# Final norm from one square per block, the forget gates' chain moved behind K's norms, and a weight tile between sums and spread at the FFN norm

## The reference

```
h = [meta; x]                                   # 528 x 1024
hn = rms_norm(h, attn_norm)
q, k, v, gate, f = split(hn @ fox_w_in)         # 16 heads of 64
q, k = rms_norm per head
c = cumsum(log_sigmoid(f + b_f))                # per head, along the tokens
s = q.k / 8 + c_q - c_k, causal                 # softmax, times v, times sigmoid(gate)
h = h + o @ fox_w_out
h = h + swiglu(rms_norm(h, ffn_norm))           # hidden width 2816
h = rms_norm(h, final_norm)[16:]                # x of the second block
n1 = rms_norm(h, norm1_g) * (1 + sc1) + sh1     # sc, sh from silu(c) @ w_ada
h = h + g1 * mixer(n1)                          # conv branch of 31 taps, state space branch
h = h + g2 * moe(rms_norm(h, norm2_g) * (1 + sc2) + sh2)   # 64 experts, top 2
out = rms_norm(h, final_g)
```

## Time and profile before

| | |
|---|---|
| median of 3 runs | 2474.2 us (2468.7 to 2475.04) |
| the profiled execution | 2477.98 us, of which the span from the first to the last instruction is 2476.2 |
| PE busy | 2295.3 us (93%), mean granted clock 0.969 |
| DVE, ACT, POOL busy | 1030.7, 723.5, 780.0 us |
| chain that ended last | PE 55%, DMA 29%, DVE 11%, ACT 3% |
| DMA | 599.45 MB, some 425 GB/s from about 1550 us on |

### The profile page before, as it was taken

One profiled execution on the slowest core, in us unless ns is written; L12 is line 12 of the kernel. 1 busy time (PEld: TensorE's weight loads), 2 busy tenths in 40 slices (PEclk: granted clock), 3 DMA queues, 4 the chain that ended last, 5 costly groups with the idle time before them and its releaser, 6 DMA issues.

```text
span 2476.2 us, 26324 instructions
## 1 busy us (share of the span) xinstructions
PE 2295.3 (93%) x10666; PEld 1436.1 (58%) x10666; DVE 1030.7 (42%) x1701; ACT 723.5 (29%) x1165; POOL 780.0 (32%) x493
## 2 busy tenths in 40 slices
PE   8999999999999999999999998988888888888885
PEld 5677678888887787777777783323233232323222
DVE  2736545543445999846675323111111111111113
ACT  4435643222224333557774231100000000100001
POOL 4235645564553343433326611111111000000100
PEclk9999999999999999999999998999999999999997
DMA  5131233644644443243444268999999999999996
GB/s 178 44 133 65 83 116 102 204 145 157 204 124 103 102 102 98 82 145 128 136 150 192 93 246 341 423 424 424 424 424 425 427 426 425 426 426 426 427 426 258
DMA packets 174776, 599.45 MB, mean 242 GB/s; under 512 B 17733, under 2 KB 96581, under 8 KB 148928
## 3 DMA queue, kind: packets, MB, share of 16 engines
q1 hardware_dynamic: 155568, 564.39, 58.7%
q10 hardware_dynamic: 8416, 23.92, 2.5%
q0 software_dynamic: 10672, 9.46, 1.2%
HBM read 593.19 MB, written 28.97 MB: 251 GB/s over the span
## 4 chain that ended last, share of the span: by engine, by line
PE 55%; DMA 29%; DVE 11%; ACT 3%; issue 1%; POOL 1%; SPq 0%; ACTq 0%; DVEq 0%; POOLq 0%
DMA arena<-in_w 21%; PE ps L828 11%; PE ps L830 11%; PE ps L829 11%; PE ps L1361 7%; DMA ring<-in_w 6%; DVE ps L2311 5%; PE ps L1359 2%; PE ps L1380 1%; PE ps L1063 1%; PE ps L879 1%; PE ps L1041 1%; PE ps L1032 1%; PE ps L929 1%; PE ps L1007 1%
## 5 line engine op out<-in xcount | busy, mean ns | idle before, releaser
L2759 POOL TENSOR_TENSOR ring_r<-ring,ring_r 128x1024 fp32r<-128x1024 f32 (+2 forms) x215 | 510.3, 2381 | 674.2 <-ACT ring_r L1455 674.0
L828 PE MATMUL ps<-r,ring_r 128*128 128x512 f32 (+2 forms) x1496 | 598.3, 400 | 1.5 <-DVE arena L2299 1.2
L830 PE MATMUL ps<-r,ring_r 128*128 128x512 f32 (+2 forms) x1496 | 585.2, 391 | 0.0
L829 PE MATMUL ps<-r,ring_r 128*128 128x512 f32 (+2 forms) x1496 | 584.9, 391 | 0.0
L1466 ACT ACTIVATE arena<-ps 128x512 f32<-128x512 f32 (+5 forms) x239 | 159.1, 688 | 1073.9 <-PE ps L1361 851.1
L1361 PE MATMUL ps<-arena 128*64 128x512 f32 x672 | 317.2, 628 | 69.5 <-DMA arena<-in_w 69.2
L1359 PE MATMUL ps<-arena 128*64 128x512 f32 x672 | 329.6, 640 | 0.0
L1455 ACT ACTIVATE ring_r<-ring 128x1024 fp32r<-128x1024 f32 x220 | 222.5, 1014 | 354.3 <-PE ps L830 201.1
L828 PEld LDWEIGHTS ps<-r,ring_r 128*128 128x128 f32 (+2 forms) x1496 | 280.8, 188 | 72.5 <-issue 11.7
L2874 POOL DMA_INDIRECT y_d<-arena,cbm x64 | 63.9, 999 | 815.7 <-DVE arena L2713 557.1
L829 PEld LDWEIGHTS ps<-r,ring_r 128*128 128x128 f32 (+2 forms) x1496 | 280.8, 188 | 63.5 <-issue 5.0
(11 more groups left out here) (377 smaller groups left out, 2612.7 us busy)
## 6 DMA issues: line engine op xcount, KB each, us to landing
arena<-in_w SPq DMA_DIRECT2D x106, 2048.0 KB, 35.9
ring<-in_w SPq DMA_DIRECT2D x86, 2048.0 KB, 37.0
ring<-in_w_ada SPq DMA_DIRECT2D x12, 2048.0 KB, 7.9
ring<-in_ffn_w_in SPq DMA_DIRECT2D x22, 1024.0 KB, 7.7
ring<-in_w_in SPq DMA_DIRECT2D x40, 512.0 KB, 6.1
ring<-in_w_in SPq DMA_DIRECT2D x8, 2048.0 KB, 9.2
ring<-in_fox_w_in SPq DMA_DIRECT2D x7, 2048.0 KB, 8.5
arena<-acs_d SPq DMA_DIRECT2D x16, 512.0 KB, 3.7
```

Source lines behind the costliest of these rows:

```text
L828: e.matmul(out, wh[:, k, :], X.hi[:, k0 + k, :], start=first and k == 0, stop=False)
L829: e.matmul(out, wh[:, k, :], X.lo[:, k0 + k, :], start=False, stop=False)
L830: m = e.matmul(out, wl[:, k, :], X.hi[:, k0 + k, :], start=False, stop=last and k == nk - 1)
L2759: e.tensor_tensor(GL[t], grans[t][1], GH[t].bitcast(F32), ALU.subtract).then_inc(sem["gr_lo"], 1)
```

## The change

Forget gates: `log1p_rest` is cut into pieces (`forget_part`) that DVE runs behind `head_norm("v", j)` for j = 4 to 7, of which only j = 4 still has a norm. `FL` moves to free space, `SEL2` is made by ACT near the start, and PE and ACT no longer wait for `cscan`. FFN norm: PE makes `hg1` between the sums and the spread, and `hu1` behind it. Final norm: ACT squares h once, one block earlier and ahead of its split, and makes `x2` itself; DVE keeps two sums of that one square, plain and weighted by final_norm² + eps (`G2E`), the last block being left to PE; PE sums the weighted row first, in two banks, then the spread, and the plain row around it; its root is taken behind n1; the fillers shrink from 10, 2 and 4 matmuls to 2 (each shows as two instructions in the trace). Four banks are taken in place of two.

```diff
@@ -232,10 +232,11 @@
     for half, (k0, nk) in enumerate(HALVES):
         for nt in range(k0, k0 + nk):
             t("hg", nt)
+            if nt == 1:
+                t("fnb")
             t("hu", nt)
             if nt == 0:
                 t("fn")
-                t("fnb")
             for n in ada_done(half, nt):
                 t("adb", n)
         for nt in range(8):
@@ -243,7 +244,9 @@
             for n in ada_out(half, nt):
                 t("adb", n)
     t("fin")
+    t("fin7")
     t("finb")
+    t("finq")
     for j in range(2):
         t("taps", j, bank=6 + j)
     taps = {6, 7}
...
-        FL = view(30656, 4, L)[0:16]
+        FL = view(23872, 4, L)[0:16]
...
+        FACC, G2E = HTM[0:2], P("attn_norm")
+
+        def square_of(name, k):
+
+            if name == "fin":
+                return FACC[0] if k == 0 else HTM[2 + k % 2]
+            return ACC if k == 0 else TMP[k % 2]
...
+            def columns_of(out, tts, *terms):
+
+                for tt in tts:
+                    for x, weight in terms:
+                        m = e.matmul(out[:, tt:tt + 1], x[:, 128 * tt:128 * tt + 128], weight, start=x is terms[0][0], stop=x is terms[-1][0])
+                return m
...
                 w.wait_ge(u.free, u.n)
-                w.wait_ge(sem["cscan"], 3)
+                w.wait_ge(sem["sc"], 3)
...
             sums_by_token("fn")
+            whole("hg", 1, X=XF)
             spread("fn", "fnb")
+            whole("hu", 1, X=XF)
             for half, (k0, nk) in enumerate(HALVES):
                 for nt in range(k0, k0 + nk):
-                    if nt > 0:
+                    if nt > 1:
                         whole("hg", nt, X=XF)
...
                             ada_columns(n)
-            fill(10, "fin")
-            sums_by_token("fin")
-            fill(2, "finb")
+            rows0, adds0, nk = sums["fin"]
+            u, u7, uq, x7 = ps("fin"), ps("fin7"), ps("finq"), square_of("fin", 7)
+            w.wait_ge(sem["sq_used"], adds0 + 2 * (nk - 2))
+            for use in (u, u7, uq):
+                w.wait_ge(use.free, use.n)
+            columns_of(u.ap, range(4), (FACC[1], ones[:, 0:1])).then_inc(u.full, 1)
+            w.wait_ge(sem["sq"], rows0 + nk)
+            columns_of(u7.ap, range(4), (x7, G2E[:, 7:8])).then_inc(u7.full, 1)
+            columns_of(uq.ap, range(2), (FACC[0], ones[:, 0:1]), (x7, ones[:, 0:1]))
             spread("fin", "finb")
-            fill(4, *conv_tiles(0)[0])
+            columns_of(uq.ap, range(2, 4), (FACC[0], ones[:, 0:1]), (x7, ones[:, 0:1])).then_inc(uq.full, 1)
+            fill(2, *conv_tiles(0)[0])

...
                 e.activation(hnH[:, k, :], TMP[k % 2][:, NM:L], ACT.Copy).then_inc(sem["hn_hi"], 1)
             w.wait_ge(sem["param"], 16)
             e.activation(SC, P("c"), ACT.Silu).then_inc(sem["sc"], 1)
+            for hh in range(2):
+                e.activation(SEL2[:, NM * hh:NM * hh + NM], C("sel16"), ACT.Copy).then_inc(sem["sc"], 1)
             w.wait_ge(sem["hn"], 8)
...
-            w.wait_ge(sem["cscan"], 1)
             next_tile()
             for nt in range(AHEAD):
...
             def squares_fin(k):
 
                 square_after(ps("fo", 1, k), "fin", k, hT[:, k, NM:L])
-                square_row("fin", k, hT[:, k, NM:L], T, 1, pc("final_norm", k))
+                if k == 7:
+                    e.activation(ST[:, 12:13], C("eps"), ACT.Sqrt)
+                e.activation(x2[:, k, :], hT[:, k, NM:L], ACT.Identity, scale=pc("final_norm", k)).then_inc(sem["x2"], 1)
...
                 for i in range(16):
+                    if half == 1 and i % 2 == 1 and i >= 3:
+                        squares_fin(i // 2 - 1)
                     next_tile()
-                    if half == 1 and i % 2 == 1 and i >= 5:
-                        squares_fin(i // 2 - 2)
-            for k in (6, 7):
-                squares_fin(k)
-            e.activation(ST[:, 12:13], C("eps"), ACT.Sqrt)
+            squares_fin(7)
             u = ps("fin")
             w.wait_ge(sem["dg"], diags["fin"] - 1)
-            w.wait_ge(u.full, u.n + 1)
-            e.activation(ST[:, 4:8], u.ap[:, 4:8], ACT.Sqrt, scale=1.0 / D, bias=C("eps2"))
-            evict(ST[:, 8:12], u, ACT.Sqrt, src=u.ap[:, 0:4], scale=1.0 / D, bias=C("eps"))
+            w.wait_ge(u.free, u.n + 1)
+            e.activation(ST[:, 4:8], ST[:, 4:8], ACT.Sqrt, scale=1.0 / D, bias=C("eps2")).then_inc(ps("fin7").free, 1)
             w.wait_ge(sem["x2"], 8)
             e.dma_start(a["x2_d"], x2).then_inc(sem["spill"], 16)
...
             for k in range(8):
                 w.wait_ge(sem["n1"], k + 1)
                 e.activation(n1H[:, k, :], TMP[k % 2][:, :T], ACT.Identity, bias=modcol(0, k)).then_inc(sem["n1_hi"], 1)
+            u = ps("finq")
+            evict(ST[:, 8:12], u, ACT.Sqrt, src=u.ap[:, 0:4], scale=1.0 / D, bias=C("eps"))
...
+                e.tensor_tensor(acc, acc, square_of(name, k)[:, :n], ALU.add).then_inc(sem["sq_used"], 1)
+
+            def add_final(k):
+
+                rows0, adds0, nk = sums["fin"]
+                x, gain = square_of("fin", k), G2E[:, k:k + 1]
+                w.wait_ge(sem["sq"], rows0 + k + 1)
+                if k == 0:
+                    e.tensor_scalar(FACC[1], x, gain, None, ALU.mult).then_inc(d.next(), 1)
+                    last()
+                    return
+                if k >= 2:
+                    w.wait_ge(sem["sq_used"], adds0 + 2 * (k - 1))
+                e.scalar_tensor_tensor(FACC[1], x, gain, FACC[1], ALU.mult, ALU.add).then_inc(sem["sq_used"], 1)
+                e.tensor_tensor(FACC[0], FACC[0], x, ALU.add).then_inc(sem["sq_used"], 1)
 
             def low(name, k, dst, src, hi, hi_sem, value):
...
                 w.wait_ge(u.free, u.n + 1)
             log1p_exp(FL[:, 0, :], FL[:, 1, :])
-            log1p_rest(FL[:, 1, :], FL[:, 2, :], FL[:, 3, :], 1)
-            e.scalar_tensor_tensor(FL[:, 1, :], FL[:, 0, :], 0.0, FL[:, 3, :], ALU.min, ALU.subtract).then_inc(d.next(), 1)
-            last()
-            e.tensor_tensor_scan(cT, C("ones", 0, 16)[:, 0:1].broadcast_to([16, L]), FL[:, 1, :], 0.0, ALU.mult, ALU.subtract).then_inc(sem["cscan"], 1)
-            w.wait_ge(sem["cscan"], 1)
-            for hh in range(2):
-                e.tensor_copy(SEL2[:, NM * hh:NM * hh + NM], C("sel16")).then_inc(sem["cscan"], 1)
+
+            def forget_part(j):
+
+                if j == 4:
+                    log1p_ratio(FL[:, 1, :], FL[:, 2, :], FL[:, 3, :], 1)
+                if j == 5:
+                    log1p_terms(FL[:, 2, :], FL[:, 3, :], 15, 13, 11, 9)
+                if j == 6:
+                    log1p_terms(FL[:, 2, :], FL[:, 3, :], 7, 5, 3)
+                if j == 7:
+                    log1p_end(FL[:, 1, :], FL[:, 3, :])
+                    e.scalar_tensor_tensor(FL[:, 1, :], FL[:, 0, :], 0.0, FL[:, 3, :], ALU.min, ALU.subtract).then_inc(d.next(), 1)
+                    last()
+                    e.tensor_tensor_scan(cT, C("ones", 0, 16)[:, 0:1].broadcast_to([16, L]), FL[:, 1, :], 0.0, ALU.mult, ALU.subtract).then_inc(sem["cscan"], 1)
+                    w.wait_ge(sem["cscan"], 1)
 
             for c in range(2):
                 for kk in range(4):
                     head_norm("v", 4 * c + kk)
+                    forget_part(4 * c + kk)
                 u = ps("vs", c)
...
                     if half == 1:
                         w.wait_ge(ps("fo", 0, nt).free, ps("fo", 0, nt).n + 1)
+                        if nt == 0:
+                            e.tensor_tensor(G2E, P("final_norm"), P("final_norm"), ALU.mult).then_inc(d.next(), 1)
+                            last()
+                            e.tensor_scalar(G2E, G2E, EPS, None, ALU.add).then_inc(d.next(), 1)
+                            last()
+                        else:
+                            add_final(nt - 1)
                     w.wait_ge(u.full, u.n + 1)
                     e.tensor_tensor(hT[:, nt, NM:L], hT[:, nt, NM:L], u.ap, ALU.add).then_inc(u.free, 1)
                     for n in ada_out(half, nt):
                         mod(n)
                     for n in ada_between(half, nt + 1):
                         ada(n)
-                    if half == 1:
-                        w.wait_ge(u.free, u.n + 1)
-                        e.tensor_scalar(x2[:, nt, :], hT[:, nt, NM:L], pc("final_norm", nt), None, ALU.mult).then_inc(sem["x2"], 1)
-                        if nt >= 3:
-                            for i in range(2):
-                                add_squares("fin", nt - 2, i=i)
-            for i in range(2):
-                add_squares("fin", 6, i=i)
-
             u = ps("adb", 3)
             w.wait_ge(u.free, u.n + 1)
             e.tensor_scalar(SC, MOD[:, 8:16], 1.0, None, ALU.add).then_inc(d.next(), 1)
             last()
             e.tensor_tensor(SC, SC, P("norm1"), ALU.mult).then_inc(d.next(), 1)
-            w.wait_ge(sem["x2"], 8)
+            w.wait_ge(sem["x2"], 7)
```

(15 more changed lines are left out.)

59 lines of the change are left out of this document (23 added, 36 removed).

## The result

The changed kernel took 2457.8 us (median of five runs, 2452.6 to 2459.3), the kernel before 2473.9 on the same chip: a ratio of 0.9938, with a 95% interval of 0.9927 to 0.9949. On a second chip, where the changed kernel ran again, it was 0.9938 as well (0.9926 to 0.9950), 2456.9 against 2472.0. The forecast was 2457, with a range of 2449 to 2466.

What follows compares the result with a forecast made beforehand. Bound by PE (55% of the span) and DMA (29%), with DVE's taps and the experts' stream only shifting. 5.8 - 0.2 + 1.8 + 10.0 = 17.4 us off the median of 2474.2 gave 2457, range 2449 to 2466.

Steps and rivals of the forecast that it cites:

- Forget gates, 5.8: V's projection: PE's wait for ACT's square and the slow matmuls behind it go, 5.8 us gained, at least 3.9.
- SEL2's copies: V's projection: two copies on ACT ahead of the third tile's split lose 0.2 us, bounds 0 and 0.4.
- What moves behind it: Behind V's projection: DVE's chain ends about 147.5, load 6 goes at most 5 us later, cover 8 us on ACT.
- The step that took c_d at 8.2: Behind the chain: even with c_d's earlier 8.2 us behind a 2 MB load, the rows are read back by 157.5.
- FFN norm, 1.8: FFN norm: 2.8 us of wait and low clock go, a 1.0 wait comes at hg2; 1.8 gained, bounds 0.3 and 2.8.
- Final norm, 10.0: Last FFN tile to the pair's end: an earlier root and fewer fillers gain 10.0 us, bounds 8.5 and 12.0.
- Sum, 17.4: Whole kernel: 5.8 - 0.2 + 1.8 + 10.0 = 17.4 us gained, the profiled execution becoming 2460.6.
- the low-clock rival: Pair behind the final norm: all 48 matmuls stay at 1.2 GHz, whole gain 8.4 us, 2466; chance 0.09.
- The early gains: Attention or FFN: a transfer or DVE takes back the first two parts' 7.4 us, 10 left, 2464; chance 0.08.
- The rival that ends slower: Load 6: SP's wait for cscan holds it until PE waits; 0.3% slower needs cscan at about 192; 2482, chance 0.03.
- ACT's table load: Final norm: 1.28 us with the dummy straight behind; with the page's 1.38 drain the gain would be some 1.4 smaller.

Runs made afterwards that it cites:

- root first: Changed kernel with the Sqrt table loaded behind tile 6's square and x2's last row behind the final norm's root; one execution, 2453.9 us.
- the pair without fillers: Changed kernel with root first, hg2's split behind the FFN root, and no two fillers ahead of the pair; pair ends 22.40 us behind the last tile.
- both edits together: Changed kernel with root first and hg2's split and Silu table load behind the FFN root, fillers kept; 2455.0 us, ratio 0.9927.

## Why the prediction was right, step by step

- **Forget gates, 5.8.** Measured 5.79 in every trace that has the part. SEL2's copies took 0.31 on ACT, and the split behind them starts 0.32 behind the operation ahead of them, before 0.11: 0.21 lost, 0.2 forecast.
- **What moves behind it.** The chain ended at 149.7, not 147.5: one operation, L2091, took 2.93 where the same one took 0.69 before. It lay beside one of POOL's splits, and so did one of the seven operations above it:
```profile
138.55 2.78 DVE L2086 SCALAR_TENSOR_TENSOR arena<-arena 16x528 f32<-16x528 f32 x1
```
```profile
138.34 2.43 POOL L2809 TENSOR_TENSOR ring_r<-ring,ring_r 128x1024 fp32r<-128x1024 f32 x1 [3.04 <-ACT ring_r L1467]
144.26 2.40 POOL L2809 TENSOR_TENSOR ring_r<-ring,ring_r 128x1024 fp32r<-128x1024 f32 x1 [3.49 <-ACT ring_r L1467]
```
The other six took 0.69 or 0.70 each. Both long operations begin behind a split's start and end 0.56 us behind its end. Before, the chain met one such split (its long operation took 2.77 at 101.19), so the chain's 16.3 us that the forecast moved held one; in its new place it meets two, and that is the 2.2 us. The step that took c_d at 8.2 erred the other way. Load 6 at 153.28 is inside the forecast's 157.5, and the split of its first tile is at 174.88, forecast 174.8. That the load landed when forecast (166.20, forecast 166) is luck: it was issued 4.2 earlier, but took 12.9 us beside the rows that were being read back, not the 8.2 that the forecast took as the most; the load before it took 8.6.
- **FFN norm, 1.8.** At `hg2` 1.97, with a wait of 0.85 where 1.0 was forecast. What the step missed: the low half of a later tile is late too. PE waits for it 0.43 in the second trace and 0.35 in the part alone; the first trace lists no second wait and comes 0.2 late at that tile. By the last tile it is 1.58 in one trace, 0.93 in the other, 1.19 alone. The mechanism was right; the term is 1.2, and runs alone can't see it (0.9999).
- **Final norm, 10.0.** 9.0 and 9.5 in the two traces, 10.0 alone. By its own path the forecast had the root 3.65 behind the tile (3.59), the diagonal done after 4.85 (4.80), the pair's first matmul after 10.35 (10.26). Its terms for the pair, 11.5 + 1.6 - 0.5 = 12.6, measured 12.67, and the 0.5 from DVE's pacing came back as 0.4: before, six of the 48 steps were 0.27 to 0.31, and now, behind eight matmuls at the low clock, all forty are PE's own 0.23. What went wrong is the addition: 767.7 + 12.6 is 780.3 and not 779.8, so this path gives 9.0, what the first trace shows, and the forecast wrote 9.5. It then took 10.0, nearer to a clock held high, which no trace shows for the whole way; the 10.0 of the part alone has a clock that fell later. That ACT's table load, dummy and x2 set the root's pace is shown by moving them (0.56 us).
- **Sum, 17.4.** 16.3 by the pair's end; the medians give 16.1 and 15.1. The forecast lies 1.3 to 2.3 above these, of which the final norm and POOL's second wait are 1 to 2. That the profiled execution, 2459.3, lies so near the forecast's 2460.6 is luck: 2.9 of its 18.7 are the router's clock.
- **The rivals.** The pair came back to 2.4 GHz after eight matmuls, so the low-clock rival fell, though its reason held: spread and pair's start are at the low level. The Trainium skill, TensorE: Matmul & The Clock Gate, What's actually happening (the low clock is the default, activity releases it) agrees. The early gains weren't given back beyond POOL's wait. The rival that ends slower has its price: with 14 us of cover and 16.3 gained, I estimate that SP would have to be held some 30 us longer for no gain and 38 for a loss of 0.3%, a scan at 188, not the 192 forecast.
- **ACT's table load.** 1.28, and its dummy straight behind, on the path or off it (745.59 and 746.88 in the moved one). The drain of 1.38 that the Trainium skill gives (ScalarE: Activation LUTs, What ACT_TABLE_LOAD costs) isn't there in either place.

Open: why the router ran at full clock in both traces of the changed kernel (20.28) and in part at the low one in that of before (23.20). It was at full clock with the forget gates alone and not with either other part alone. Of ten traces with the forget gates' part eight are at full clock; root first and the pair without fillers (22.32 both) are not, though both edits together are (20.28). In these two the stretch ahead of the router is shorter, 60.6 us from SP's first load of an expert to the router's mark in place of 63.9, with a granted clock of 1.00 in its first 15.5 us in root first where the changed kernel has 0.78. So it isn't shown to belong to any part, and the medians speak against it: the forget gates alone gave 5.3, under the 5.8 of their own step.

## What to carry to other kernels

An engine that takes its work in order is held by whatever stands ahead in its queue: look at the order of two cheap instructions (a square and a split that waits for a slot, a root and a scaling nobody needs yet) before their cost, and don't count a lead of some tiles as cover when the same engine serves another chain.

Behind a wait that is removed, follow the next producer for more than one tile; POOL was late a second time in two of three traces.

Where one profile differs from the next by more than the medians do, cut both at the same marks and see in which stretches the difference lies before it is credited to the change.

## What was not expected of the hardware

- TensorE's granted clock differs between executions of one and the same kernel at the same instruction. In the changed kernel's two traces the block behind the convolution ran at 0.91 in one and 1.00 in the other. The final norm of before took 31.93 us, and 33.15 and 30.74 in kernels with the same instructions there. With the new norm and its two fillers the pair behind it has 3 to 10 matmuls at the low clock, by the trace. A start that lies 2 us earlier or later (V's first group at 94.05 to 95.93), the two places between pair and experts (3.6 us together) and the router (2 to 3) are together about the size of the 7 to 9 us by which runs of one kernel differ; that they are its cause isn't shown.
- On one-column matmuls PE is busy and yet the clock falls: in the kernel with fillers ahead of the spread it fell during the columns, which follow a tile at 2.4 GHz and a wait of 0.66 us (eight instructions took 1.70 us, against 1.03).
- A merged row can hide one long operation. The seven of L2086 took 7.16 us, as before (7.15), but six of them took 0.69 or 0.70 and one 2.78. All three long operations, two now and one before, begin while a split of POOL runs and end 0.55 or 0.56 us behind its end (138.55 + 2.78 against 138.34 + 2.43, 144.28 + 2.93 against 144.26 + 2.40, and before 101.19 + 2.77 against 100.66 + 2.74). The chain's reciprocal was not slowed: 3.44 us, with a split that began 1.21 behind its start, and 3.44 before.
